# First block's mixer: differential logits first, latent ones late, rows turned without diagonals

## What is computed

```python
def hybrid_mixer(x, w_in, q_norm, kv_norm, w_uq, w_uk, w_uv, lam_params, diff_norm, w_o,
                 cos, sin, bias_dist, lambda_init):
    h = x @ w_in
    c_q, c_kv, k_r, dq, dk, dv = jnp.split(h, splits, axis=-1)
    q = (rms_norm(c_q, q_norm, 1e-6) @ w_uq).reshape(b, s, MLA_HEADS, MLA_NOPE + MLA_ROPE)
    q_nope = q[..., :MLA_NOPE]
    q_rope = apply_rope(q[..., MLA_NOPE:], cos[None, :, None], sin[None, :, None])
    c_kv = rms_norm(c_kv, kv_norm, 1e-6)
    k_nope = (c_kv @ w_uk).reshape(b, s, MLA_HEADS, MLA_NOPE)
    v_mla = (c_kv @ w_uv).reshape(b, s, MLA_HEADS, MLA_V)
    k_rope = apply_rope(k_r, cos[None], sin[None])
    mla_out = mla_attention(q_nope, q_rope, k_nope, k_rope, v_mla).reshape(b, s, MLA_HEADS * MLA_V)
    lam = jnp.exp(jnp.sum(lp[0] * lp[1])) - jnp.exp(jnp.sum(lp[2] * lp[3])) + lambda_init
    d_out = diff_attention(dq, dk, dv, bias_dist, lam)      # softmax 0 minus lam times softmax 1
    d_out = rms_norm(d_out, diff_norm, 1e-5) * (1.0 - lambda_init)
    merged = jnp.concatenate([mla_out, d_out.reshape(b, s, DIFF_HEADS * DIFF_V)], axis=-1)
    return merged @ w_o
```

## Time and profile before

| | us |
|---|---|
| median of 3 runs (lowest, highest) | 2449.84 (2446.45, 2450.92) |
| the profiled execution | 2448.96 |
| its span | 2447.2 |
| mixer 0: first matmul, last matmul of its output projection | 13.86, 184.61 |
| mixer 1: the same | 389.78, 544.47 |
| busy: TensorE, VectorE, ScalarE | 2215.9, 1792.3, 1390.1 |

### The profile page before, as it was taken

One profiled execution on the slowest core, in us unless ns is written; L12 is line 12 of the kernel. 1 busy time (PEld: TensorE's weight loads), 2 busy tenths in 40 slices (PEclk: granted clock), 3 DMA queues, 4 the chain that ended last, 5 costly groups with the idle time before them and its releaser, 6 DMA issues.

```text
span 2447.2 us, 31120 instructions
## 1 busy us (share of the span) xinstructions
PE 2215.9 (91%) x12576; PEld 1938.3 (79%) x12576; DVE 1792.3 (73%) x2375; ACT 1390.1 (57%) x1808; POOL 43.6 (2%) x20
## 2 busy tenths in 40 slices
PE   7879999877999999999999999776789998779998
PEld 6768998766888888888888888565689977569997
DVE  4447556556999999999999999667666665657665
ACT  3325444435878777777777777444454454244444
POOL 0002002001000000000000000000000000000000
PEclk9879999987999999999999999878899998889999
DMA  7314654334999999999999999433245543115552
GB/s 272 112 52 160 202 190 136 131 121 150 376 350 376 356 361 350 363 356 359 352 364 352 361 354 364 150 112 109 86 155 188 190 156 124 35 52 190 189 177 104
DMA packets 280527, 546.65 MB, mean 223 GB/s; under 512 B 8500, under 2 KB 114104, under 8 KB 280248
## 3 DMA queue, kind: packets, MB, share of 16 engines
q1 hardware_dynamic: 277336, 535.86, 62.1%
q10 hardware_dynamic: 3040, 8.72, 1.0%
HBM read 543.49 MB, written 1.05 MB: 223 GB/s over the span
## 4 chain that ended last, share of the span: by engine, by line
PE 84%; DVE 10%; ACT 3%; DMA 1%; issue 1%; SPq 0%; DVEq 0%; ACTq 0%
PE psum L394 18%; PE psum L395 17%; PE psum L396 17%; PE psum L388 8%; PE psum L390 8%; PE psum L389 8%; PE psum L1398 1%; DVE wl L377 1%; PE psum L571 1%; DMA raw<-in_w_in 1%; PE psum L1418 1%; ACT arena L550 1%; PE psum L594 1%; PE psum L1408 1%; ACT XT L423 1%
## 5 line engine op out<-in xcount | busy, mean ns | idle before, releaser
L377 DVE TENSOR_TENSOR wl<-raw,wh 128x1024 fp32r<-128x1024 f32 (+1 forms) x640 | 771.6, 1230 | 219.4 <-ACT wh L369 214.4
L369 ACT ACTIVATE wh<-raw 128x1024 fp32r<-128x1024 f32 (+1 forms) x640 | 661.6, 1050 | 310.5 <-PE psum L390 149.6
L388 PE MATMUL psum<-xh,wh 128*128 128x256 f32 x1600 | 464.0, 290 | 26.3 <-DVE wl L377 18.9
L377 DVE TENSOR_TENSOR wl<-arena,wh 128x1024 fp32r<-128x1024 f32 x384 | 458.2, 1221 | 32.5 <-ACT wh L369 23.8
L394 PE MATMUL psum<-wh,xh 128*128 128x512 f32 (+1 forms) x1152 | 460.8, 400 | 21.3 <-DVE xl L407 16.2
L389 PE MATMUL psum<-xl,wh 128*128 128x256 f32 x1600 | 460.0, 288 | 0.0
L390 PE MATMUL psum<-xh,wl 128*128 128x256 f32 x1600 | 459.7, 287 | 0.0
L369 ACT ACTIVATE wh<-arena 128x1024 fp32r<-128x1024 f32 x384 | 404.5, 1062 | 94.4 <-PE psum L396 94.4
L395 PE MATMUL psum<-wl,xh 128*128 128x512 f32 (+1 forms) x1152 | 453.7, 394 | 0.0
L396 PE MATMUL psum<-wh,xl 128*128 128x512 f32 (+1 forms) x1152 | 453.5, 394 | 0.0
L388 PEld LDWEIGHTS psum<-xh,wh 128*128 128x128 f32 x1600 | 315.2, 197 | 31.6 <-DVE wl L377 14.8
(11 more groups left out here) (318 smaller groups left out, 1721.0 us busy)
## 6 DMA issues: line engine op xcount, KB each, us to landing
arena<-in_moe_g SPq DMA_DIRECT2D x72, 1024.0 KB, 7.0
arena<-in_moe_u SPq DMA_DIRECT2D x72, 1024.0 KB, 7.6
raw<-in_moe_d SPq DMA_DIRECT2D x64, 1024.0 KB, 7.2
arena<-in_moe_d SPq DMA_DIRECT2D x48, 1024.0 KB, 6.9
raw<-in_ff_up SPq DMA_DIRECT2D x48, 1024.0 KB, 5.2
raw<-in_moe_g SPq DMA_DIRECT2D x40, 1024.0 KB, 7.5
raw<-in_moe_u SPq DMA_DIRECT2D x40, 1024.0 KB, 7.1
raw<-in_ff_down SPq DMA_DIRECT2D x24, 1024.0 KB, 4.8
```

What stands on the lines that cost most here:

```text
L369: A.activation(unit(s, i)[0], raw_half(s, i), ACT.Copy).then_inc(*s.w_hi.tick(i))
L377: V.tensor_tensor(lo, raw_half(s, i), hi.bitcast(F), SUB).then_inc(*s.w_lo.tick(i))
L388: T.matmul(ps, wh, x[0][:, k, :], start=k == 0, stop=False)
```

## The change

- The weights come in another order: in3 to in6 first, then in0 to in2, dv, uq, ukv; of the output projection o2, o3 (the differential half) before o0, o1.
- The differential logits are computed right after in3 to in6 and one unit of in0. The two softmaxes are joined on unnormed exponentials by VectorE: row 0 plus (sum 0 times minus lambda over sum 1) times row 1 (join). The joined rows are turned by a plain transpose (turn_heads), copied, and multiplied so that the values come out by rows. The sums of squares are taken there by ScalarE, per row; the inverse root on VectorE takes the place of the softmax sum too (roots, the 1e-5 of the norm is multiplied by the sum squared). Then the normed values are transposed (turn_diff) and split (turned).
- The latent columns are split without their factor, straight from PSUM, ScalarE the high and VectorE the low part. The factor of the queries goes into the scale of the logits (rq), that of keys (KS) and values (in the copy VM) behind the up projections.
- The latent logits come after all up projections. Their rows are normed by VectorE (normal) and turned by transposes; turning and values stand between the first four steps of the output projection, which begins with the differential half and waits per row half (ready).
- The bias table is made between in3 and in6 of mixer 0; its two transfers are issued by POOL (pool_bias) instead of SyncE.
- PSUM is claimed and released bank by bank (take, empties), pairs are still there.
- The four arena slots wait for four different points of mixer 1.
- The other users of pe_project (second block) pass the waits that they had.

The diff, cut to its core:

```diff
-        for c in range(4):
+        for c in (3, 4, 5, 6, 0, 1, 2):
...
+        for n in (2, 3, 0, 1):
...
-                Y.wait_ge(*pe.of("m1.ds" if q == NS + 2 else "m1.d5.av"))
+                Y.wait_ge(*pe.of(("m1.T1", "m1.dav1", "m1.aT0", "m1.aav1")[q - NS]))
...
+        for n in range(4):
+            T.wait_ge(*main.w_lo.of(us[n]))
             for t in range(2):
+                T.wait_ge(*ready(order[n], t))
                 for h in range(2):
-                    i = step(kk, t, h, unit(main, u))
-            i.then_inc(*pe.tick(("unit", u)))
-            if kk in between:
-                between[kk]()
-        if "half" in between:
-            between["half"]()
+                    i = step(n, t, h)
...
+        def turn_heads(E, W, banks, name, hs=range(4)):
+            nb = W // P
+            for h in hs:
+                for kb in range(nb):
+                    o = (h * nb + kb) * P
+                    x = T.transpose(bk(banks[o // 512])[:, o % 512:o % 512 + P], E[:, h, kb * P:(kb + 1) * P], ident)
+            x.then_inc(*pe.tick(name))
...
+        proj(3, 0, ("m0i", "f0ln")[l])
+        empties(0, (act, f"{st}.dq0"))
+        if l == 0:
+            T.wait_ge(*consts_in.of("all"))
+            T.matmul(take(4)[0:4, 0:384], S("relb")[0:32, :], C("oh")[0:32, :], start=True, stop=True
+                     ).then_inc(*pe.tick("bias.r4"))
+            empties(4, (dve, "bias.r4"))
+        T.matmul(take(5)[:, 0:2], C("ones")[0:64, 0:128], LAM[0:64, 0:2], start=True, stop=True).then_inc(*pe.tick(f"{st}.lam"))
+        empties(5, (act, f"{st}.elam"))
+        proj(4, 1)
+        empties(1, (act, f"{st}.dq1"))
+        proj(5, 2)
+        empties(2, (dve, f"{st}.dk0"))
+        if l == 0:
+            ps = claim(3)
+            T.wait_ge(*tz_in.of("tz"))
+            for n in range(2):
+                x = T.matmul(ps[:, n * 512:(n + 1) * 512], C("anti"), flat(CC[:, 2 * n:2 * n + 2, :]), start=True, stop=True)
+            x.then_inc(*pe.tick("bias.tz"))
+            drained(3, (dve, "bias.tz"))
+        proj(6, 3)
+        empties(3, (act, f"{st}.dk1"))
+        c4 = take(4)
+        chunk(0, 0, c4)
+        T.wait_ge(*act.of(f"{st}.dq1"))
+        T.wait_ge(*act.of(f"{st}.dk1"))
+        T.wait_ge(*dve.of(f"{st}.dk0"))
+        logits_diff(0, 0)
+        logits_diff(0, 1)
+        chunk(0, 1, c4)
+        empties(4, (dve, f"{st}.y0"))
+        logits_diff(1, 0)
+        c5 = take(5)
+        chunk(1, 0, c5)
+        logits_diff(1, 1)
+        chunk(1, 1, c5)
+        empties(5, (dve, f"{st}.y1"))
+        proj(2, 6)
+        empties(6, (dve, f"{st}.krt"))
...
+                    T.wait_ge(*dve.of(f"{st}.E0"))
+                    take(0)
+                    turn_heads(DE[0][0], P, (0,), f"{st}.T0")
+                    empties(0, (act, f"{st}.dPT0"))
...
+        T.wait_ge(*dve.of(f"{st}.ss.r"))
+        ps = take(1)
+        spread(ps[:, 0:256], scales_at(2), 1, 1)
+        T.wait_ge(*dve.of(f"{st}.krt"))
+        T.matmul(ps[:, 256:512], C("fold"), KRT, start=True, stop=True).then_inc(*pe.tick(f"{st}.sp"))
...
+        T.wait_ge(*dve.of(f"{st}.y0"))
+        T.wait_ge(*dve.of(f"{st}.y1"))
+        for _ in up(2, 0):
+            pass
+        drained(2, (act, f"{st}.qT"))
+        T.wait_ge(*dve.of(f"{st}.E1"))
+        claim(0)
+        turn_heads(DE[1][0], 256, (0, 1), f"{st}.T1")
+        empties(0, (dve, f"{st}.dPT1"))
+        empties(1, (act, f"{st}.dPT1"))
...
+        second = up(3, 1)
+        av_diff(0)
+        next(second)
+        av_diff(1)
+        next(second)
+        drained(3, (dve, f"{st}.qR"))
...
+        turn_diff(0)
+        ps, w = claim(2), unit(main, uv)
...
+        take(6)
+        T.wait_ge(*act.of(f"{st}.qT"))
+        T.wait_ge(*dve.of(f"{st}.kT"))
+        logits_mla(0, (6,))
+        turn_diff(1)
+        claim(0)
+        logits_mla(1, (0, 1))
...
+        pe_project(st, (1, 2), XX, lambda kk, t: dve.of(f"{st}.d{t}" if kk > 3 else f"{st}.a{t}"),
+                   {1: turn0, 2: turn1, 3: lambda: av_mla(1, 7)},
+                   lambda t: pe_turn(f"{st}ln", ar(0, 2, 1024), (0, 3), t), [4, 5, 6, 7, 0, 1, 2, 3])
...
+        def join(t):
+            _, s0, w, _ = soft_cols(2 * t)
+            _, s1, c, r1 = soft_cols(2 * t + 1)
+            V.wait_ge(*act.of(f"{st}.e{2 * t + 1}"))
+            V.reciprocal(r1, s1).then_inc(*dve.tick())
+            V.scalar_tensor_tensor(w, s0, 1e-5, s0, MUL, MUL).then_inc(*dve.tick())
+            V.wait_ge(*dve.last())
+            V.scalar_tensor_tensor(c, s0, LAM[:, 4:5], r1, MUL, MUL).then_inc(*dve.tick())
+            V.wait_ge(*dve.last())
+            for h in range(4):
+                V.scalar_tensor_tensor(DE[t][0][:, h, :], DE[t][1][:, h, :], c[:, h:h + 1], DE[t][0][:, h, :], MUL, ADD
+                                       ).then_inc(*dve.tick(f"{st}.E{t}"))
...
+                V.scalar_tensor_tensor(YL[:, c, :], bk(b)[:, i * 256:(i + 1) * 256], sc, YH[:, c, :].bitcast(F), MUL, SUB
+                                       ).then_inc(*dve.tick(f"{st}.y{n}"))
...
+            V.scalar_tensor_tensor(v, ss, 1.0 / 128, w, MUL, ADD).then_inc(*dve.tick())
+            rsqrt(y, v, x1, hv)
+            V.wait_ge(*dve.last())
+            for h in (0, 1):
+                V.tensor_scalar(DZ[t][:, h * P:(h + 1) * P], bk(2 + t)[:, h * P:(h + 1) * P], y[:, h:h + 1], None, MUL
+                                ).then_inc(*dve.tick(f"{st}.dz{t}"))
...
+        V.tensor_tensor(KT, heads(pair(0), 4), KS.unsqueeze(1).to_broadcast([P, 4, 256]), MUL).then_inc(*dve.tick(f"{st}.kT"))
+        lo_to(main, U + 28)
+        turned(0)
+        lo_to(main, U + 29)
...
+            maximum(f"am{t}", f"al{t}", 4 + t, AE[t], ps, rq[:, t, 0:1], mask_m(W))
...
+            V.tensor_tensor(AE[t], AE[t], r.unsqueeze(2).to_broadcast([P, 4, P * (t + 1)]), MUL).then_inc(*dve.tick(f"{st}.aE{t}"))
...
+        latent_max(0)
+        turned(1)
+        latent_max(1)
+        lo_to(main, U + 30)
+        normal(0)
+        lo_to(main, U + 31)
+        normal(1)
+        lo_to(main, U + 32)
...
+    def pool_bias():
+        G.wait_ge(*dve.of("bias.r4"))
+        G.dma_start(d["scratch"], R4[0:4, :]).then_inc(*tz_in.tick("r4"))
+        G.wait_ge(*tz_in.of("r4"))
+        G.dma_start(CC, bass.AP(tensor=base.tensor, offset=base.offset, ap=[[1, P], [384, 4], [1, 256]])
...
+        pool_bias()
...
-        load_to(main, main.w.ld["m0.o0"])
-        sync_bias()
```

596 lines of the change are left out of this document (332 added, 264 removed).

## The result

The changed kernel takes 2355.32 us, median of 4 runs (2353.63 to 2357.48), and the kernel before on the same chip 2449.68 us, median of 4 (2446.45 to 2450.92). The ratio is 0.9617 with a 95% interval of 0.9601 to 0.9634, so 94 us less. I forecast 2367 us and 2354 to 2395: the sign, the mechanism and the range held, and the gain was 12 us larger than forecast. The profiled execution of the changed kernel took 2355.06 us with a span of 2353.3 us, against 2448.96 and 2447.2 before.

A forecast was written before the change was run, and what follows sets the result against it. Latency bounds the mixers: TensorE waits in program order behind chains over VectorE and ScalarE. Idle time, clock and work less new waits and slips: 35.3 us (mixer 1) plus 47.2 (mixer 0), 82.5 off 2448.96, so 2367 us; range 2354 to 2395.

The forecast's parts named there:

- idle time, net: TensorE's waits in the mixers, 28.2 and 22.3 us, go, less the walk's 1.9, slips and mixer 0's table and weight-load waits.
- less work: TensorE in each mixer: fewer diagonal products, thin sums and spreads, against 32 added transposes; 8.3 us less.
- clock: The mixers' whole loss to lowered TensorE clock goes: 18.6 us in mixer 0, 10.6 us in mixer 1.
- outside the mixers: Norm and router behind each mixer and the second block are the same code; no gain counted there.
- The walk: Mixer 1 in new program order with before's durations: 113.5 us of TensorE work, 1.9 us idle, last matmul at 115.5.
- The keys' factor: Mixer 1's latent logits need keys with their factor, ready at 82.6 with TensorE free at 81.6: 1.0 us wait.
- the output projection: In mixer 1 it waits for differential half 1 turned and split: 89.0 against 88.1, 0.9 us.
- I choose 4 us per mixer for it: Allowance for late hops between engines, which the walk did not price; about a fifth of the old idle time.
- The bias table: Mixer 0's fetch from POOL, 1.33 + 3.94 us on quiet DMA engines; wait of 0 to 23 us, taken as 1.5.
- The rival: Bias table late in mixer 0 through start loads and POOL: 10 us late gives 2378, at the bound 2391; chance 0.11.
- Without waits over some 1 us I let the whole lowered clock go: In the mixers the clock falls only around long waits, so all 10.6 and 18.6 us return.
- My third rival: Mixers' clock stays low in part through transposes and short waits: half the old loss, 14.6 us, stays, 2382; chance 0.05.

The follow-up runs named there:

- latent rows: Changed kernel with the turned rows and values of the latent attention put ahead of the output projection in both mixers: 2374.81 us, ratio 0.9695.
- keys' factor: Changed kernel with two extra VectorE passes over 128x1024 (2.5 us, result unused) ahead of the keys' factor in each mixer: 2368.56 us.
- latent factor: Changed kernel with the latent norm's factor put ahead of the up projections by stand-in passes with unused results: 2377.09 us, ratio 0.9701.
- some work: Changed kernel with each of the two mixers' 64 transposes made as a full-precision product with the identity: 2364.30 us, ratio 0.9655.
- the loose place: Changed kernel with two extra VectorE passes over 128x1024 (2.5 us, result unused) ahead of the join of the first differential rows in each mixer: 2358.24 us.
- the repeats: Changed kernel profiled again with nothing edited, twice: 2359.23 us (ratio 0.9635) and 2361.40 us (ratio 0.9634).

## Why the prediction was right, and where it was off

Term by term (predicted, measured in the profiles; work and clock are the estimate from the stretches at 1.2 GHz):

| | mixer 1 | mixer 0 |
|---|---|---|
| idle time, net | 22.3 - 1.9 - 4 = 16.4, 21.5 | 20.3, 24.5 |
| less work | 8.3, 9.1 | 8.3, 9.6 |
| clock | 10.6, 9.8 | 18.6, 15.0 |
| sum | 35.3, 40.4 | 47.2, 49.1 |
| outside the mixers | 0, 4.4 for both | |

The experiments put back a part of the latency (latent rows, keys' factor, latent factor) and some work. That the early differential logits and the joined rows gave the rest is read from the waits that are gone, not from a run of their own.

**The walk.** Its last matmul of mixer 1 was at 115.5 us, against 114.25 measured. That it came so near is in part luck. The walk had 113.5 us of work at full clock; measured are 113.55 us busy, of which 4.07 at 1.2 GHz, so about 111.5 at full clock. The work was priced 2.0 us too high and the waits 1.2, and the lowered clock at the mixer's start, which the walk did not have, gave 2.0 back. That VectorE and ScalarE suffice in order, and that joined rows and normed rows are in time, held: 5 us of extra VectorE work in the loose place cost no wait. It named both remaining waits. The keys' factor was to cost 1.0 us and cost 0.6; the output projection 0.9, and cost 0.14. Both are real: taking the first away uncovered 1.1 us of the second.

**The step that failed** is "I choose 4 us per mixer for it", the allowance for slips. It is 8 of the 12 us by which I was off. Nothing slipped: the walk had no price for hops between engines, but it had priced each VectorE instruction at its full duration, and in the trace the next one often starts a tenth of a microsecond before the last one's record ends, which probably pays for the hops. In the rest, idle time was 1.3 us better than even that, the work 2.1 us better, the clock 4.4 us worse, and 4.4 us came from outside the mixers, where the repeats show nearly as much scatter: the gain over the forecast there is luck.

**The bias table** was priced by the quiet middle of the kernel at 1.33 + 3.94 us with 1.5 us of wait; it took 6.58 + 5.85 us, and 2.2 to 2.8 us of wait in the eight profiles in which its code is the changed kernel's. The rival (10 us late) did not come, but its condition, the loads at the start, was right: the read too was near its quiet 3.94 us only where the share of the DMA engines was 0.65. In a transfer of a few KB the time among the loads was not in proportion to its size. The rival's rule from the Trainium skill, "SBUF — State Buffer", section "SBUF: two separate sides", was that VectorE instructions in a two-port mode lock out the cores that write the descriptors of a transfer issued from GpSimd. The write took no less from SyncE (7.33 us), so for it the rule decides nothing; the read was 1.9 us longer from POOL, which fits the rule, a slower queue and the larger share of loads beside it alike: no run here tells them apart.

**Clock.** "Without waits over some 1 us I let the whole lowered clock go" was 4.4 us too much by the estimate above, and the reason was only half of it: 1.7 us stayed in mixer 0 behind the table's wait and 2.0 at the start of mixer 1. Added waits did bring the clock down. Right behind a wait of 3.2 us stood a stretch of 3.4 us at 1.2 GHz, a cost of 1.7 us, and over the end of waits of 4.7 and 5.7 us one of 6.8 us, in which TensorE was busy for 4.8 to 6.0 us, a cost of 2.4 to 3.0. The busy time grew by more or less than that, 1.3 to 4.9 us, since other low stretches came or went with it. But the thin bundle does it without a wait: in 10 of the 26 mixers that I have profiles of with the new order, TensorE's granted clock fell to 1.2 GHz at the end of its sums or within 1.3 us behind it, for 3.4 us, at a cost of 1.7 us. My third rival, that transposes and short waits hold the clock down, came in part: it named 14.6 us, and the transposes are not shown to be the reason. The Trainium skill's rule that a transpose does not count as activity ("TensorE: Matmul & The Clock Gate", "Part 4: PE-mode transpose") is not needed to explain what is seen: in the kernel before the clock fell behind twenty sums without a transpose, and behind the bundles of 4 and 8 transposes further on it never fell without an added wait ahead. With products in place of the transposes it did not fall behind the bundle in either mixer, nor in 14 mixers with transposes, so that says nothing. The sums alone can do it; whether the transposes add to it, and what decides when, is open.

## What to carry to other kernels

When TensorE waits in program order behind chains over two other engines, walk the new order with the old durations and note each chain's slack; the walk here was within 1.3 us in 114, in part by errors that cancelled, and needed no lump for slips. A removed wait can return as the next-tightest chain, so look up its slack first (0.6 us bought here uncovered 1.1). When a transfer is moved to another queue, look at what that queue no longer issues meanwhile: the read that seemed faster had fewer loads beside it. Once TensorE is full, judge edits of 3 us by windows around the edited code and repeat the profile of the unedited kernel, since the granted clock elsewhere moved the total by as much.

## What I had not expected of the hardware

- The changed kernel itself, in three series of runs, has medians of 2355.32, 2359.23 and 2361.40 us, single runs from 2353.63 to 2361.67; the kernel before stayed at 2449.3 to 2450.4. In the profiles the difference is in how long the clock is low in code that is the same.
- A write of 6 KB took 1.33 us with quiet DMA engines (share 0.02) and 5.1 to 6.6 us from POOL's queue and 7.3 us from SyncE's among the loads of the start (shares of 1.01 to 1.07).
- Twenty one-column matmuls without a pause, with four transposes behind them or with none, can be followed by 3.4 us at 1.2 GHz.
